# One core, two decoder layers: when the S5 matrices are loaded and built, and which ring slot a load takes

## The reference

```python
# layer 0
z = h @ w_in                              # 3368 columns: q, k, v of A and B, and an indexer
o = concat([diff_attention(A), dsa_attention(B)]) @ w_out
# layer 1
z = h @ w_in                              # 2048 columns: q, k, v of C, and u of the S5 part
dt = exp(log_dt)                          # one per channel group, 32 of them
abar = exp(lam_re * dt) * (cos(lam_im * dt) + i sin(lam_im * dt))     # 32 groups x 64 states
bbar = (abar - 1) / lam * b               # 32 x 64 x 16, complex
h_t = abar * h_(t-1) + bbar @ u_t ;  y_t = Re(c @ h_t) + d * u_t
o = concat([moba_attention(C), glu(gelu(y))]) @ w_out
# both layers, after the mixer
top-1 of 4 groups, top-2 of 8 experts: silu(x @ w1) * (x @ w3) @ w2
# shift, scale and gate around each part: c @ ada_w + ada_b
```

## Time and profile before

| | |
|---|---|
| time before, median of 3 runs | 1529.83 us (1529.28 to 1530.37) |
| the profiled execution: its time | 1531.76 us |
| the profiled execution: span | 1530.0 us |
| PE busy | 1322.5 us (86%) |
| DVE busy | 431.4 us (28%) |
| ACT busy | 217.9 us (14%) |
| POOL busy | 105.6 us (7%) |
| moved by DMA | 493.46 MB, mean 323 GB/s |
| chain that ended last | PE 48%, DMA 39%, DVE 7% |

### The profile page before, as it was taken

One profiled execution on the slowest core, in us unless ns is written; L12 is line 12 of the kernel. 1 busy time (PEld: TensorE's weight loads), 2 busy tenths in 40 slices (PEclk: granted clock), 3 DMA queues, 4 the chain that ended last, 5 costly groups with the idle time before them and its releaser, 6 DMA issues.

```text
span 1530.0 us, 15107 instructions
## 1 busy us (share of the span) xinstructions
PE 1322.5 (86%) x6157; PEld 662.5 (43%) x6157; DVE 431.4 (28%) x888; ACT 217.9 (14%) x458; POOL 105.6 (7%) x128
## 2 busy tenths in 40 slices
PE   5889989699989988988967865978999899899897
PEld 2334468544334433433435323875343343343333
DVE  3164663721111111110135715253211111111112
ACT  1123241111101110110100004211111010110100
POOL 1110000300300300300000000000000000000000
PEclk8999959699999999999988977779999999999999
DMA  9998521159999999999991097113999999999993
GB/s 371 222 371 344 205 125 55 55 213 430 428 429 427 427 429 427 429 427 428 428 399 63 1 377 310 49 61 116 420 428 428 428 428 426 428 428 428 428 427 159
DMA packets 51801, 493.46 MB, mean 323 GB/s; under 512 B 4744, under 2 KB 5968, under 8 KB 20880
## 3 DMA queue, kind: packets, MB, share of 16 engines
q1 hardware_dynamic: 48816, 488.33, 76.8%
q0 software_dynamic: 1056, 0.89, 1.2%
q10 hardware_dynamic: 1856, 3.20, 0.6%
HBM read 489.25 MB, written 3.15 MB: 322 GB/s over the span
## 4 chain that ended last, share of the span: by engine, by line
PE 48%; DMA 39%; DVE 7%; issue 2%; ACT 2%; SPq 1%; DVEq 0%; POOLq 0%; POOL 0%; PEldq 0%; ACTq 0%
DMA ring<-in_moe_w 34%; PE B L735 19%; PE B L572 5%; PE A L652 4%; PE B L752 3%; PE B L585 3%; DMA ring<-in_ev_w_in 2%; PE B L707 2%; PE B L529 2%; DMA ring<-in_ada_w 2%; PE A L762 2%; PE B L518 2%; PE B L622 1%; PE B L951 1%; DVE work L1030 1%
## 5 line engine op out<-in xcount | busy, mean ns | idle before, releaser
L735 PE MATMUL B<-ring,work 128*64 128x512 f32 x2048 | 475.4, 618 | 62.6 <-DMA ring<-in_moe_w 60.3
L735 PEld LDWEIGHTS B<-ring,work 128*64 128x64 f32 x2048 | 159.5, 142 | 340.5 <-issue 339.1
L752 PE MATMUL B<-ring,work 128*64 128x512 f32 x1024 | 231.8, 594 | 1.2 <-ACT work L1678 1.2
L1301 DVE TENSOR_TENSOR work<-work,B 64x512 f32<-64x512 f32 x64 | 68.1, 1065 | 506.8 <-ACT work L1674 506.3
L752 PEld LDWEIGHTS B<-ring,work 128*64 128x64 f32 x1024 | 75.9, 137 | 137.2 <-issue 137.2
L1674 ACT ACTIVATE work<-B 64x512 f32<-64x512 f32 x64 | 37.7, 589 | 621.5 <-PE B L735 621.5
L762 PE MATMUL A<-work 128*128 128x256 f32 x512 | 118.1, 384 | 8.9 <-DVE work L1307 8.9
L1885 POOL COPY work<-work 128x512 f32 x62 | 38.2, 617 | 1106.3 <-PE B L735 744.8
L762 PEld LDWEIGHTS A<-work 128*128 128x128 f32 x512 | 94.6, 190 | 28.5 <-issue 16.9
L572 PE MATMUL B<-ring,hT 128*128 128x512 f32 (+1 forms) x224 | 96.8, 593 | 5.6 <-DVE hT L1081 3.3
L1307 DVE COPY work<-B 64x512 f32<-64x512 f32 x64 | 43.7, 684 | 117.4 <-PE B L752 117.4
(11 more groups left out here) (248 smaller groups left out, 940.5 us busy)
## 6 DMA issues: line engine op xcount, KB each, us to landing
ring<-in_moe_w SPq DMA_DIRECT2D x192, 2048.0 KB, 19.9
ring<-in_ada_w SPq DMA_DIRECT2D x24, 2048.0 KB, 20.5
ring<-in_ev_w_in SPq DMA_DIRECT2D x6, 2048.0 KB, 22.0
ring<-in_od_w_in SPq DMA_DIRECT2D x4, 2048.0 KB, 19.4
ring<-in_ev_w_out SPq DMA_DIRECT2D x2, 2048.0 KB, 8.1
ring<-in_od_w_out SPq DMA_DIRECT2D x2, 2048.0 KB, 11.0
s_tables<-hT ACTq DMA_DIRECT2D x8, 256.0 KB, 9.5
ring<-s_tables SPq DMA_DIRECT2D x1, 2048.0 KB, 24.6
```

The costliest lines, as they stand in the source:

```text
L735: ins = pe.matmul(B5[64 * m:64 * m + 64, :], xs[:, k, :], w[:, k, :], start=(k == 0), stop=(k == KD - 1))
L752: ins = pe.matmul(B7[64 * m:64 * m + 64, :], hidTb[:, q % 2, k, :], w[:, k, 512 * m:512 * m + 512], start=(k == 0), stop=(k == KF - 1))
L1301: dve.tensor_tensor(hid[64:128, q % 2, :].rearrange("p (k q) -> p q k", k=KF), silu_a[64:128, q % 2, :].rearrange("p (q k) -> p q k", k=KF ...
```

## The change

Four things are done together.

1. log_dt is loaded as one row behind `PARAMS` and is spread by two small matmuls; ACT takes its exponential straight from PSUM. The two lam loads go out right behind it, under a semaphore of their own.
2. The loads of b, c, d and the gate's bias go out when A's q and k have been transposed (unit `A3`). DVE builds the matrices behind `out_rows_a(1, 16)` and ahead of `residual(0, 0)`; PE transposes them behind `out_proj(0, 0)` and ahead of the MoE, and ACT copies them behind `norm_root(1)`. They lie elsewhere in `work`.
3. The router's loads go out by layer, each when the last load of that layer's output projection has landed.
4. `stream()` takes the slot whose content is used up first. The content of a slot ranks by its number in the list; only the table ranks just behind layer 1's last input piece. Up to `("ada", 1, 6)` every load has the slot it had.

```diff
+def used_rank(n):
+    return N_MIX1 + LOADS1.index(("in", 3)) + 0.5 if n == N_MIX1 + LOADS1.index(("tab",)) else n
...
     for n in range(N_ALL):
-        s = n % RING
+        s = n if n < RING else min(last, key=lambda x: used_rank(last[x]))
...
-        PARAMS += [(nm, HD) for nm in ("a_lq1", "a_lk1", "a_lq2", "a_lk2")]
+        PARAMS += [(nm, HD) for nm in ("a_lq1", "a_lk1", "a_lq2", "a_lk2")] + [("s5_log_dt", 32)]
...
-        for g_ in range(2):
-            S5_PARAMS.append((logdt[64 * g_:64 * g_ + 64, :],
-                           a["s5_log_dt"][0].rearrange("(j g) -> g j", g=2)[g_].partition_broadcast(64), True))
...
@@ parameter_rows, PE
+                for g in range(2):
+                    ins = pe.matmul(A4[64 * g:64 * g + 64, 2, 0:16], ones[0:1, 0:64], prow[:, PROWS - 32 + g:PROWS:2], start=True, stop=True)
                 ins.then_inc(par_rows, 1)
@@ PE
+            def s5_transposes():
+                for v in range(4):
+                    tr_unit(f"bt{v}", [Bd[:, v, 4 * q4:4 * q4 + 4, :].rearrange("p a b -> p (a b)") for q4 in range(4)],
+                            [(p5_bt, 1)])
+                for v in range(2):
+                    tr_unit(f"ct{v}", [Cd[:, v, q4, :] for q4 in range(4)])
+                direct_term()
...
                 if q == 4:
-                    for v in range(4):
-                        tr_unit(f"bt{v}", [Bd[:, v, 4 * q4:4 * q4 + 4, :].rearrange("p a b -> p (a b)") for q4 in range(4)],
-                                [(p5_bt, 1)])
-                    for v in range(2):
-                        tr_unit(f"ct{v}", [Cd[:, v, q4, :] for q4 in range(4)])
-                    direct_term()
                     ada_columns(0, 2)
...
                 out_proj(0, s)
+            s5_transposes()
             moe(0)
@@ DVE
             out_rows_a(1, 16)
+            s5_matrices()
             residual(0, 0)
@@ ACT
+            act.wait_ge(par_rows, 1)
+            act.activation(s5p[:, 2, :], A4[:, 2, 0:16], ACT.Exp).then_inc(p5_dt, 1)
...
             norm_root(1)
+            for v in range(4):
+                tr_evac(f"bt{v}", BT[:, v // 2, v % 2], 4)
...
             moe(0)
@@ POOL
-            pool.wait_ge(h_ready, 2)
+            for dst, src, slow in LAM_PARAMS:
+                pool.dma_start(dst, src, allow_slow_non_contiguous=slow).then_inc(in_lam, 16)
+            def router_parameters(l):
+                n = n_of(l, "out", 0)
+                pool.wait_ge(slot_full[slot(n)], fills(n))
+                for dst, src, slow in ROUTER_PARAMS[l]:
+                    pool.dma_start(dst, src, allow_slow_non_contiguous=slow).then_inc(in_router[l], 16)
+            router_parameters(0)
+            pool.wait_ge(tr_ev, U["A3"] + 1)
             for dst, src, slow in S5_PARAMS:
                 pool.dma_start(dst, src, allow_slow_non_contiguous=slow).then_inc(in_s5, 16)
-            pool.wait_ge(z_ready, 6)
```

More of the change, by code:

```diff
@@ L284, in build @@
         slot_used = sem("slot_used")
-        in_cst, in_x, in_c, in_par, in_late = sem("in_cst"), sem("in_x"), sem("in_c"), sem("in_par"), sem("in_late")
+        in_cst, in_x, in_c, in_par, in_lam = sem("in_cst"), sem("in_x"), sem("in_c"), sem("in_par"), sem("in_lam")
+        in_router = [sem(f"in_router{l}") for l in range(LAYERS)]
         in_brow, par_rows, par_ready = sem("in_brow"), sem("param_rows"), sem("params_ready")
@@ L866, in _ @@
                     ada_rows(0, 1)
-                    tr_unit("lam", [s5row[:, :]], [(in_s5, 16 * N_S5)])
+                    tr_unit("lam", [s5row[:, :]], [(in_lam, 16 * len(LAM_PARAMS))])
                 if q == 2:
@@ L1410, in _ @@
             LRE, LIM, DT, TH, ARG, MAG, K, TURN, TC, SN, CS, ABR, ABI, DEN, CRE, CIM, T1, T2, AR, MAG2 = range(20)
-            dve.wait_ge(in_s5, 16 * N_S5)
             dve.wait_ge(tr_ev, U["lam"] + 1)
@@ L1471, in _, with s5_matrices @@
-            tell(p5_bt)
+            def s5_matrices():
+                dve.wait_ge(in_s5, 16 * N_S5)
+                cre = q(CRE).unsqueeze(2).to_broadcast([P, 16, 16])
+                cim = q(CIM).unsqueeze(2).to_broadcast([P, 16, 16])
+                tt(Bbar[:, 0], s5b[:, 0], cre, ALU.mult)
+                tt(Btmp, s5b[:, 1], cim, ALU.mult)
+                tt(Bbar[:, 0], Bbar[:, 0], Btmp, ALU.subtract)
+                tt(Bbar[:, 1], s5b[:, 1], cre, ALU.mult)
+                tt(Btmp, s5b[:, 0], cim, ALU.mult)
+                tt(Bbar[:, 1], Bbar[:, 1], Btmp, ALU.add)
+                are = q(AR).unsqueeze(2).to_broadcast([P, 16, 16])
+                aim = q(ABI).unsqueeze(2).to_broadcast([P, 16, 16])
+                aB = s5b
+                tt(aB[:, 0], Bbar[:, 0], are, ALU.mult)
+                tt(Btmp, Bbar[:, 1], aim, ALU.mult)
+                tt(aB[:, 0], aB[:, 0], Btmp, ALU.subtract)
+                tt(aB[:, 1], Bbar[:, 1], are, ALU.mult)
+                tt(Btmp, Bbar[:, 0], aim, ALU.mult)
+                tt(aB[:, 1], aB[:, 1], Btmp, ALU.add)
+                link(dve.memset(Bd, 0.0))
+                for v in range(2):
+                    for gp in range(2):
+                        dve.tensor_copy(Bd[64 * gp:64 * gp + 64, v, :, 16 * gp:16 * gp + 16], Bbar[64 * gp:64 * gp + 64, v])
+                        link(dve.tensor_copy(Bd[64 * gp:64 * gp + 64, 2 + v, :, 16 * gp:16 * gp + 16], aB[64 * gp:64 * gp + 64, v]))
+                    for gp in range(2):
+                        ts(Cd[:, v, :, 64 * gp:64 * gp + 64], s5c[:, v], C("par")[:, gp:gp + 1], (1.0, -1.0)[v], ALU.mult, ALU.mult)
+                tell(p5_bt)
@@ L1753, in _ @@
                     act.copy(s5p[:, 0:2, :], passed("lam")[:, 0:32].rearrange("p (a b) -> p a b", a=2)).then_inc(tr_ev, 1)
-                    act.activation(s5p[:, 2, :], logdt[:, :], ACT.Exp).then_inc(p5_dt, 1)
                     act.wait_ge(p5_arg, 1)
@@ L1769, in _ @@
                 if q == 4:
-                    for v in range(4):
-                        tr_evac(f"bt{v}", BT[:, v // 2, v % 2], 4)
-                    for v in range(2):
-                        tr_evac(f"ct{v}", CT[:, v], 4)
-                    tr_evac("k0", K0[:, :, :].rearrange("p a b -> p (a b)").unsqueeze(1), 1)
                     ada_evac(0, "c2")
@@ L1799, in _ @@
             norm_root(1)
+            for v in range(4):
+                tr_evac(f"bt{v}", BT[:, v // 2, v % 2], 4)
+            for v in range(2):
+                tr_evac(f"ct{v}", CT[:, v], 4)
+            tr_evac("k0", K0[:, :, :].rearrange("p a b -> p (a b)").unsqueeze(1), 1)
             moe(0)
@@ L1823, in gate @@
                 if j == GATE_AT + 1:
-                    act.wait_ge(in_late, 16 * N_LATE)
+                    act.wait_ge(in_s5, 16 * N_S5)
                     act.wait_ge(glu_done, 1)
@@ L1889, in _ @@
                     phases(0)
+                else:
+                    router_parameters(1)
                 pool.wait_ge(start_ready, l + 1)
```

58 lines of the change are left out of this document (17 added, 41 removed).

## The result

| | before | after |
|---|---|---|
| median beside each other | 1529.55 us (1528.52 to 1530.37) | 1481.15 us (1480.88 to 1481.82) |
| ratio, 95% interval | | 0.9686, 0.9671 to 0.9702 |
| the profiled execution: its time | 1531.76 us | 1481.32 us |
| its span | 1530.0 us | 1479.4 us |
| mean granted clock of TensorE | 0.917 | 0.936 |

The gain is 48.4 us by the medians, where 38.8 were forecast, so the forecast fell short by 9.6 us.

What follows compares the result with a forecast made beforehand. The MoE was taken as bound by reading experts, the mixers by PE's waits. Terms 13.6 + 5.4 - 0.4 + 20.2 = 38.8 us gave 1493.0 us from the profiled execution, 1491.0 against the median; range 1484 to 1499.

Steps and rivals of the forecast that it cites:

- Term A: Layer 0's adaLN rows and input projection: without early S5 loads PE's four waits and slow stretch go, 13.6 us gained.
- rival of an early stall that stays: Layer 0: low rate has another cause or the wait moves to piece 2; 13.6 us lost, 1504.6 us, chance 0.06.
- Term B: Layer 0's input projection: S5 transposes taken out of PE's chain of waits, 5.4 us gained.
- Term C: Layer 0, ahead of the residual: DVE builds the matrices there, making PE wait for the first square; cost 0.4 us.
- S5 transposes ahead of the MoE: Layer 0, before the router: seven units fit PE's 6.98 us idle time; cost 0, without that cover 5.4 us.
- Term D: Layer 1's input projection: new slot choice removes waits of 14.94 and 1.77 us and their clock loss, 20.2 us gained.
- The clock between projection and MoE: Layer 0's router: transposes filling PE's idle gap might keep the clock up, 0 to 3.5 us; taken as 0.
- the rival: Clock stays up through the transposes before layer 0's router: up to 3.5 us more, 1487.5 to 1490, chance 0.17.
- with some room for the clock elsewhere: Last step, whole kernel: widened the first three cases' 1487.5 to 1496.4 us to a range of 1484 to 1499 us.

Runs made afterwards that it cites:

- the run with the row: Kernel before with only log_dt loaded as one row and spread by two small matmuls, in place of two element-wise loads; 1516.14 us, ratio 0.9895.
- the filled wait: Kernel before with 12 unread matmuls in TensorE's 3.1 us wait in layer 1's attention; 1524.26 us, ratio 0.9964.
- the tanh gate: Changed kernel with layer 1's S5 gate computed by tanh and one VectorE operation in place of the sigmoid; 1482.21 us.
- the run with 6 unread matmuls: Changed kernel with 6 matmuls that nobody reads in the 3.1 us wait of layer 1's attention; 1478.62 us, ratio 0.9672.

## Why the prediction was wrong

- **Term A**, 13.6 forecast, 14.1 found; its cause, log_dt alone, is shown by the run with the row, which gains the same 14.1 us up to piece 5. The rival of an early stall that stays is out.
- **Term B**, 5.4 forecast, 5.4 found.
- **Term C**, -0.4 forecast, 0.0 found. DVE's matrices were costed at their old duration, 12.8 us. In the new place they took 11.4 us. Four of the eight small copies had taken 0.46 to 0.67 us at 101.6 to 105.9 us, the others 0.27 to 0.29; now all eight take 0.28 or 0.29. At the old place POOL issued the router's loads from 101.07 us on; at the new one it issues none. In the run with the log_dt row both come earlier together (POOL from 85.6, copies from 87.6 us, up to 0.53 us each). That POOL's issues slow the copies fits this, but no run tried it by itself.
- **S5 transposes ahead of the MoE**, 0 forecast and found, with 1.40 us to spare; the b and c loads landed 12 to 16 us after their issue, and DVE did not wait for them.
- **Term D**, 20.2 forecast, 19.9 found.
- **The clock between projection and MoE**, taken at 0, was 1.1 us. The router's matmuls took 6.07 in place of 7.04; up to the first expert another 1.3 us was lost to the clock again, and 0.8 of waiting and 0.6 of clock gained. PE's busy time by stretch shows the clock full while it did little but transposes, 58% busy, and falling soon after:

```profile
248.70:256.00 7.30, 4.22 (x90) 1.00 0.56 239
256.00:266.00 10.00, 7.72 (x44) 0.72 0.01 2
```

  So it neither stayed up, as the rival had it, nor was it at half all through, as before. The Trainium skill (TensorE: Matmul & The Clock Gate, Part 4: PE-mode transpose) says that transposes do not count as PE being busy in the same way; these rows, a fall that comes late, do not decide that rule.
- **The step that failed** is the last one, "with some room for the clock elsewhere". The sum took clock into account only for instructions right behind a removed wait, and left 3 us or so at either side for the rest. In the profiled executions the rest was 9.9 us: 7.5 in layer 1's attention and output projection, whose instructions the change leaves alone, 0.3 elsewhere, and 2.1 in layer 0 that belong to one late execution of the kernel before. That the 7.5 us are clock is shown by the filled wait, which gives 6.3 of them to the kernel before. The changed kernel, 43 us earlier there, stands at a place where the clock comes back sooner; that is in part luck of the place: delays of 0.7 to 3.6 us took 2.5 to 8 us of the total away again, beside their own length, and the best places of both kernels are 43 us apart. Whether the 4.4 us that remain on the mean over the delays would vanish over more places stays open.

Open is why the half-clock stretch of the attention lasts 7 us at one place in time and 10, 17 or 24 at others, while PE works through nearly all of it, and what starts the later fall where the 3.1 us wait is gone. So is why layer 0's output projection starts between 212.5 and 216.4 us in kernels that are the same up to there, and why the kernel before spreads over 2 to 10 us from one set of runs to the next where the changed one spreads over 1 to 2.

## What to carry over

Look for single-element loads beside a weight stream: two of 4 KB cost 14 us here, and a row and two small matmuls replace them. Where a ring serves a buffer that is kept for long, let the load behind it take the slot that comes free next. And in a kernel whose clock falls and returns within its stages, a shift alone moves the time: a range needs this kernel's own swing (here 3 to 8 us) on both sides, and a change should be judged over several small delays. An idle wait inside dense work is worth filling as a trial, no longer than the wait.

## Hardware behaviour that was not expected

- 2.2 us of added delay made one kernel 4 us faster and another 10 us slower. In the first, "to out(1, 0)" fell by 5.5 us with the granted clock; in the second, the trace shows 2.5 us of clock there, and the longer executions were not traced.
- A wait of 3.1 us in otherwise dense work had the clock fall in it, or up to 1.7 us behind it, for 7 to 24 us at 1.2 GHz; 2.9 us of unread matmuls in it kept 2.4 GHz. With the wait cut to 0.96 us by the tanh gate, or filled by 5.45 us of matmuls, the changed kernel had 7 us at 1.2 GHz later.
- At half clock PE works through this attention without a wait (transposes of a unit 1.06 us, products 1.81, in the kernel before); at full clock it waits for ACT between (0.61 and 1.10, with waits of 0.4 to 1.1 us, in the run with 6 unread matmuls).
- Two loads of 4-byte elements, 4 KB each, held the whole stream at 68 GB/s for 12 us, though POOL issued them on another queue; without them 414 GB/s.
